# A Strassen feed-forward whose block products are fed in another order on each engine, with a fourth raw weight buffer

## The reference

```python
def swiglu(x, w_in, w_out):
    gate, up = jnp.split(x @ w_in, 2, axis=-1)
    return (jax.nn.silu(gate) * up) @ w_out
```

## Time and profile before

| | |
|---|---|
| time, median of 3 runs | 3603.94 us (3603.62 to 3606.51) |
| profiled execution | 3605.75 us, span 3603.9 us, mean granted clock 0.933 |
| busy share | PE 88%, DVE 55%, ACT 38%, POOL 37% |
| weight transfers, feed-forward inputs | 176 x 512 KB |
| HBM | 251 MB read, 70 GB/s over the span |

### The profile page before, as it was taken

How to read it: one execution, slowest core, us unless ns; L and a number is a source line. 1 busy time by engine, 2 the same in 40 slices (tenths; PEclk the granted TensorE clock), 3 DMA queues, 4 the chain that set the end, 5 groups by cost and what they waited for, 6 DMA issues and landing times.

```text
span 3603.9 us, 50073 instructions
## 1 busy us (share of the span) xinstructions
PE 3179.4 (88%) x20476; PEld 2679.7 (74%) x20476; DVE 1992.3 (55%) x3148; ACT 1383.3 (38%) x2398; POOL 1316.0 (37%) x971
## 2 busy tenths in 40 slices
PE   6999999999997988998998798887888999979787
PEld 4877677777777777866777787877777885678776
DVE  2255483266747464675546645576455617474645
ACT  3331373342643333433444323353233417443323
POOL 2233323335245334263213442424424343353432
PEclk9999999999998999997779899898999999989998
DMA  5212202211021221230001212122121320112222
GB/s 222 88 65 106 93 1 66 94 50 55 19 75 64 81 100 65 77 105 30 8 2 65 80 62 99 64 83 83 70 88 66 98 94 12 53 40 90 77 84 75
DMA packets 74163, 256.73 MB, mean 71 GB/s; under 512 B 8016, under 2 KB 11216, under 8 KB 72784
## 3 DMA queue, kind: packets, MB, share of 16 engines
q1 hardware_dynamic: 73072, 248.82, 20.3%
q0 software_dynamic: 864, 4.72, 0.4%
HBM read 251.41 MB, written 2.10 MB: 70 GB/s over the span
## 4 chain that ended last, share of the span: by engine, by line
PE 61%; DVE 16%; POOL 7%; issue 6%; DMA 5%; ACT 5%; SPq 0%; ACTq 0%; DVEq 0%; POOLq 0%
PE banks L439 59%; DMA w_raw<-in_l_ffn_w_in 4%; DVE area L1502 2%; PE banks L448 2%; POOL w_lo L405 2%; ACT w_hi L390 1%; DVE w_lo L416 1%; DVE w_last L410 1%; DVE w_lo L405 1%; POOL area L1497 1%; POOL w_sum L431 1%; POOL w_sum L425 1%; DVE area L1508 1%; POOL w_sum L429 1%; POOL w_sum L427 1%
## 5 line engine op out<-in xcount | busy, mean ns | idle before, releaser
L439 PE MATMUL banks<-area,w_hi 128*128 128x256 f32 (+3 forms) x6892 | 1709.4, 339 | 215.3 <-ACT area L1449 126.2
L439 PEld LDWEIGHTS banks<-area,w_hi 128*128 128x128 f32 (+2 forms) x6892 | 1195.1, 194 | 396.4 <-ACT area L1449 134.8
L439 PE MATMUL banks<-area,w_lo 128*128 128x256 f32 (+3 forms) x3446 | 1150.7, 336 | 0.0
L405 POOL TENSOR_TENSOR w_lo<-w_raw,w_hi 128x1024 fp32r<-128x1024 f32 (+1 forms) x179 | 416.5, 2329 | 914.5 <-ACT w_hi L390 914.5
L439 PEld LDWEIGHTS banks<-area,w_lo 128*128 128x128 f32 (+2 forms) x3446 | 668.9, 194 | 69.7
L439 PE MATMUL banks<-area,w_late 128*128 128x256 f32 (+2 forms) x2766 | 510.5, 338 | 58.0 <-ACT area L1449 48.7
L439 PEld LDWEIGHTS banks<-area,w_late 128*128 128x128 f32 (+1 forms) x2766 | 428.5, 197 | 119.7 <-ACT area L1449 51.7
L390 ACT ACTIVATE w_hi<-w_raw 128x1024 fp32r<-128x1024 f32 (+2 forms) x271 | 269.5, 1001 | 568.2 <-PE banks L439 282.9
L439 PE MATMUL banks<-area,area 64*64 64x32 f32 (+11 forms) x4424 | 402.4, 316 | 66.3 <-DMA area<-in_w_mod 16.4
L439 PEld LDWEIGHTS banks<-area,area 64*64 64x64 f32 (+4 forms) x4424 | 309.4, 174 | 147.7 <-issue 57.6
L405 POOL TENSOR_TENSOR w_late<-w_raw,w_late 128x1024 fp32r<-128x1024 f32 (+1 forms) x45 | 110.6, 2458 | 324.1 <-ACT w_late L390 324.1
(11 more groups left out here) (286 smaller groups left out, 3708.4 us busy)
## 6 DMA issues: line engine op xcount, KB each, us to landing
w_raw<-in_l_ffn_w_in SPq DMA_DIRECT2D x176, 512.0 KB, 3.4
w_raw<-in_w_in SPq DMA_DIRECT2D x66, 512.0 KB, 3.6
w_raw<-in_l_ffn_w_out SPq DMA_DIRECT2D x64, 512.0 KB, 4.1
w_raw<-in_w_mod SPq DMA_DIRECT2D x32, 512.0 KB, 4.6
w_raw<-in_l_ffn_w_out SPq DMA_DIRECT2D x32, 384.0 KB, 3.1
w_raw<-in_w_qkv SPq DMA_DIRECT2D x24, 512.0 KB, 3.3
w_raw<-in_l_w_in SPq DMA_DIRECT2D x22, 512.0 KB, 3.3
w_raw<-in_w_out SPq DMA_DIRECT2D x32, 320.0 KB, 2.9
```

Source lines behind the costliest of these rows:

```text
L405: e.tensor_tensor(lo, raw_of(m), hi.bitcast(f32), SUB).then_inc(*sig(name, "weights", m, kind))
L439: return e.matmul(out, lhsT, rhs, start=first, stop=stop, skip_group_check=True)
```

## The change

- **Raw buffers.** The angle tables (cos, sin) move to the start of the constants' tile. Once layer 1 has used them for the last time, their 128x1024 serve as a fourth raw buffer; a piece goes to the buffer that was filled longest ago. It is named `const` in the changed kernel.
- **Order of split tiles.** "last" of a unit comes ahead of the next unit's s12 and s34. At a phase's end it comes behind the first output piece; that piece, "last" and the second output piece get their remainders from GpSimd instead of VectorE.
- **ScalarE in a unit.** The p1 copy comes first, then the next unit's gate piece, this unit's s34, silu, u2, "last", the next unit's s12, and the rounding of a.
- **VectorE in a unit.** The s34 remainder moves from the end of the unit before to behind c11; the others follow c22, "last" first.
- **GpSimd.** The fourth sum comes before the third, and the s12 remainder waits for the fourth only. It goes on with the second unit's weights before the last t remainder.
- **Entry of a layer.** VectorE makes two of the t remainders (0 and 1) and both weight remainders before it scales the plain tiles; the third plain tile is worked inside the first unit.
- **Output projection.** All k tiles but the last two, of output tiles 0 and 1, are taken first.

No instruction's size changes. The code (indentation cut by eight, the body of `round_one` is that of the old loop):

```diff
-for _name, _n in (("ident", 128), ("ones", 128), ("head_ones", 128), ("rot", 128), ("eps", 2),
-          ("cos", 512), ("sin", 512), ("upper", 256), ("pick", 128),
+for _name, _n in (("cos", 512), ("sin", 512), ("ident", 128), ("ones", 128), ("head_ones", 128), ("rot", 128), ("eps", 2),
+          ("upper", 256), ("pick", 128),
...
-            ents += [(n, "plain"), (n, "s12")]
-            if ents[-3][1] == "s34":
-                ents.append((ents[-3][0], "last"))
-            ents.append((n, "s34"))
-        elif order[n + 1][0] != name:
-            ents.append((n - 1, "last"))
+            ents.append((n, "plain"))
+            if ents[-2][1] == "s34":
+                ents.append((ents[-2][0], "last"))
+            ents += [(n, "s12"), (n, "s34")]
     elif split:
+        after_units = len(ents) > 0 and ents[-1][1] == "s34"
         ents.append((n, "whole"))
+        if after_units:
+            ents.append((ents[-2][0], "last"))
 ent_at = {ent: k for k, ent in enumerate(ents)}
+end_ents = {k + i for k, (n, kind) in enumerate(ents) if kind == "s34" and ents[k + 1][1] == "whole" for i in (1, 2, 3)}
...
+over_angles = piece_no["l0_ffn1_w_in", 0]
+raw_sb.append(const)
+raw_slots, last_raw = [], [None] * N_RAW
+for n in range(len(order)):
+    if n == over_angles:
+        last_raw.append(None)
+    oldest = min(range(len(last_raw)), key=lambda i: (last_raw[i] is not None, last_raw[i] or 0, i))
+    raw_slots.append((oldest, last_raw[oldest]))
+    last_raw[oldest] = n
+
 def raw_of(n):
-    return raw_sb[n % N_RAW][:, 0:ins[order[n][0]].shape[-1]]
+    return raw_sb[raw_slots[n][0]][:, 0:ins[order[n][0]].shape[-1]]
...
-    if n >= N_RAW:
-        q.wait_ge(*at("raw free", n - N_RAW))
-    e.dma_start(raw_of(n), ins[order[n][0]][order[n][1]]).then_inc(*sig(f"raw{n % N_RAW}", "raw", n, by=16))
+    slot, before = raw_slots[n]
+    if before is not None:
+        q.wait_ge(*at("raw free", before))
+    elif slot == N_RAW:
+        q.wait_ge(*at(layer1.late.tag, "q", "cos", 3))
+        q.wait_ge(*at(layer1.late.tag, "q", "sin", 3))
...
+        round_one(q, e, q.w - 1)
+
+def round_one(q, e, k):
...
-        if kind == "whole" and dve == ("ffn" in order[m][0] or m in last_leads) or (kind == "plain" and not dve):
+        if (kind == "whole" and dve == (("ffn" in order[m][0] or m in last_leads) and k not in end_ents)
+                or (kind == "plain" and not dve)):
...
-        if kind == "last" and dve:
+        if kind == "last" and dve == (k not in end_ents):
...
-            q.wait_ge(*at("weight sums", m, "s34"))
+            q.wait_ge(*at("fourth sum", m))
...
-                e.tensor_tensor(s3, g0, u0, SUB).then_inc(*sig("w_sums"))
                 q.wait_ge(*at("weight sums", m, "s12"))
-                e.tensor_tensor(s4, g1, s2, SUB).then_inc(*sig("w_sums", "weight sums", m, kind))
+                e.tensor_tensor(s4, g1, s2, SUB).then_inc(*sig("w_sums", "fourth sum", m))
+                e.tensor_tensor(s3, g0, u0, SUB).then_inc(*sig("w_sums", "weight sums", m, kind))
...
+            after.t_hi_act(q, e, 0)
         norm.squares.root(q, e, 0)
...
+                lead=[(m, k) for m in range(2) for k in range(j1 - j0 - 2)],
...
-        for i in (0, 1):
-            self.t_hi_act(q, e, i)
-        self.silu_act(q, e, 0)
+        self.t_hi_act(q, e, 1)
+        round_to(q, e, self.ent(DIRECT, "s12"))
         self.t_hi_act(q, e, 2)
-        self.silu_act(q, e, 1)
-        round_to(q, e, self.ent(DIRECT, "s12"))
-        self.a_hi_act(q, e, 0)
-        self.a_hi_act(q, e, 1)
-        self.silu_act(q, e, 2)
-        self.t_hi_act(q, e, 3)
-        round_to(q, e, self.ent(DIRECT, "s34"))
-        self.a_hi_act(q, e, 2)
+        round_to(q, e, self.ent(DIRECT, "s34") + 1)
         for p, out in enumerate(self.outs):
             units = self.units(p)
             for u in units:
                 unit_end = self.ent(u, "s34")
-                more = u < units[-1]
-                if more:
-                    round_to(q, e, unit_end + 1)
                 q.wait_ge(*at(self.tag, "product", u, "p1"))
                 if u - 2 in units:
                     q.wait_ge(*at(self.tag, "c11", u - 2))
                 e.activation(self.p1[u % 2], self.quarter(u, 0), ACT.Copy).then_inc(
                     *sig("ffn_p1", self.tag, "p1", u))
+                if u == DIRECT:
+                    for v in (0, 1):
+                        self.silu_act(q, e, v)
+                else:
+                    round_one(q, e, unit_end + 1)
+                    if q.w <= unit_end:
+                        round_one(q, e, unit_end)
+                    q.w = unit_end + 2
                 if u > units[0]:
                     self.silu_act(q, e, u - 1)
                 q.wait_ge(*at(self.tag, "product", u, "p6"))
@@ -1455,10 +1475,17 @@
                     q.wait_ge(*at(self.tag, "c21", u - 2))
                 e.activation(self.u2[u % 2], self.quarter(u, 0), ACT.Copy).then_inc(
                     *sig("ffn_u2", self.tag, "u2", u))
-                round_to(q, e, unit_end + (3 if more else 1))
+                if u == DIRECT:
+                    for v in (0, 1):
+                        self.a_hi_act(q, e, v)
+                    self.t_hi_act(q, e, 3)
+                round_to(q, e, unit_end + 3)
+                if u == DIRECT:
+                    self.silu_act(q, e, 2)
                 if u > units[0]:
                     self.a_hi_act(q, e, u - 1)
-                round_to(q, e, unit_end + (4 if more else 3))
+                elif u == DIRECT:
+                    self.a_hi_act(q, e, 2)
             self.silu_act(q, e, units[-1])
             self.a_hi_act(q, e, units[-1])
...
+        self.t_lo_dve(q, e, 0)
+        self.last_combined_dve(q, e)
+        self.t_lo_dve(q, e, 1)
+        rest_to(q, e, self.ent(DIRECT, "s34"), dve=True)
         self.norm.scaled(q)
         for u in (0, 1):
             q.wait_ge(*at("evicted", self.project.group(2 * u, 0)))
             e.tensor_tensor(self.sg[u], self.sg[u], self.norm.rs, MUL).then_inc(
                 *sig("lead_scaled", self.tag, "gate", u))
-        self.t_lo_dve(q, e, 0)
         for u in (0, 1):
             q.wait_ge(*at("evicted", self.project.group(2 * u + 1, 0)))
             e.tensor_tensor(self.a[u], self.a[u], self.norm.rs, MUL).then_inc(
                 *sig("lead_scaled", self.tag, "scaled", u))
         for u in (0, 1):
             self.product_dve(q, e, u)
-        self.last_combined_dve(q, e)
-        for u in (0, 1):
-            self.a_lo_dve(q, e, u)
+
+    def third_dve(self, q, e):
+
         q.wait_ge(*at("projected", self.project.group(4, 0)))
         q.wait_ge(*at(self.tag, "product", 0))
         e.tensor_tensor(self.sg[0], self.project.bank(4, 0), self.norm.rs, MUL).then_inc(
             *sig("evicted_dve", "evicted", self.project.group(4, 0)))
         also(self.tag, "gate", 2)
-        rest_to(q, e, self.ent(DIRECT, "s12"), dve=True)
+        self.a_lo_dve(q, e, 0)
         q.wait_ge(*at("projected", self.project.group(5, 0)))
         q.wait_ge(*at(self.tag, "a", 0))
         e.tensor_tensor(self.a[0], self.project.bank(5, 0), self.norm.rs, MUL).then_inc(
             *sig("evicted_dve", "evicted", self.project.group(5, 0)))
         also(self.tag, "scaled", 2)
-        self.product_dve(q, e, 2)
-        rest_to(q, e, self.ent(DIRECT, "s34"), dve=True)
-        self.a_lo_dve(q, e, 2)
+        self.a_lo_dve(q, e, 1)
 
...
-                more = u < units[-1]
...
+                rest_to(q, e, unit_end, dve=True)
...
-                if not more:
-                    rest_to(q, e, unit_end + 1, dve=True)
+                if u == DIRECT:
+                    self.third_dve(q, e)
                 if u > units[0]:
                     self.up_dve(q, e, u - 1)
...
-                rest_to(q, e, unit_end + (3 if more else 2), dve=True)
+                rest_to(q, e, unit_end + 3, dve=True)
                 if u > units[0]:
                     self.a_lo_dve(q, e, u - 1)
-                rest_to(q, e, unit_end + (4 if more else 3), dve=True)
+                elif u == DIRECT:
+                    self.product_dve(q, e, 2)
+                    self.a_lo_dve(q, e, 2)
...
         rest_to(q, e, self.ent(DIRECT, "s34"))
-        for i in (1, 2, 3):
-            self.t_lo_dve(q, e, i, "t_lo_pool")
+        self.t_lo_dve(q, e, 2, "t_lo_pool")
+        rest_to(q, e, self.ent(DIRECT + 1, "s34"))
+        self.t_lo_dve(q, e, 3, "t_lo_pool")
         for p, out in enumerate(self.outs):
-            rest_to(q, e, self.ent(self.units(p)[-1], "last"))
+            rest_to(q, e, self.ent(self.units(p)[-1], "last") + 1)
```

23 lines of the change are left out of this document (12 added, 11 removed).

## The result

The changed kernel takes 3466.6 us (median of 4 runs, 3463.3 to 3471.6) against 3605.2 us for the kernel before beside it: ratio 0.9613, 95% interval [0.9595, 0.9631]. The forecast was 3470. The profiled execution took 3471.55 us (span 3469.8), 134 less than the one before.

The account below looks back on a forecast made before the run. TensorE waits for product 1's copy behind a transfer-bound rounding; afterwards VectorE and GpSimd's shared port bounds units. Savings 28.6 + 0.8 + 3.9 = 33.3 us a layer, 133 in four, give 3470 us; eight-in-ten range 3415 to 3545.

Parts of the forecast that it names:

- entry and phase one: Layer start: entry gains 0.8 us; phase one's copies span 49.8 us (first interval 11.65, then three unit intervals) instead of 56.15.
- phase two: Second group of units in a layer: 9.5 us plus six unit intervals, 85.7 us instead of 99.08.
- phase three: Third group of units in a layer: 9.5 us plus four unit intervals, 60.3 us instead of 69.17.
- output projections (A, B, rest): Last copy of phase one (A) or two (B) to next phase's first, and remaining span: net 1.3 us a phase, 3.9 a layer.
- P: Time of one feed-forward unit in the new order, 12.7 us, between a floor of 11.7 and a ceiling of 15.2.
- 3345 us: Time claimed if VectorE and GpSimd did not exclude each other at the shared port: units of some 10.3 us, time near 3345.
- 12 to 13 us apart: Sign that the forecast is right: the spacing of the product-1 copies in the units.
- other five signs: Copy wait nearly gone; VectorE's 128x1024 remainders often 2 us; TensorE awaits s12, s34; no ScalarE feed-forward transfer waits; entries wait 10 us.
- Both break the loop: Units: fourth raw buffer and product-1 copy ahead of the rounding each break the 15 us transfer loop; the 3.5 us wait goes.
- 4.0 us: First interval of a layer: the new entry order shortens it from 15.65 to 11.65 us.
- with GpSimd splitting the first output tiles the second goes: Output projection start: the second of three TensorE waits, 0.78 us for the first output weights, disappears.
- will often wait a little: Product 7 of a phase's last unit, before the output projection: small waits, allowed for in the net 1.3 us a phase.

Follow-up runs that it names:

- e4: Changed kernel with GpSimd's sum S3 = g0 - u0 replaced by a copy of g0, subtraction left out: ratio 0.9432 to the kernel before; two slow executions not used.
- e8: Changed kernel with the gate piece's 128x1024 remainder on VectorE instead of GpSimd, except in each phase's first unit: 3432.75 us, ratio 0.9521 to the kernel before.
- e3: Kernel before with the fourth raw buffer only, all its orders kept: 3456.61 us, ratio 0.9572 to the kernel before.
- e5: Kernel before with only ScalarE's product-1 copy put ahead of the rounding, three raw buffers: 3611.79 us, ratio 1.0007 to the kernel before.
- e1: Changed kernel with three raw buffers instead of four, all its orders kept: 3503.17 us, ratio 0.9703 to the kernel before.
- e12: Changed kernel with the remainders of a phase's last three pieces back on VectorE: 3445.79 us, ratio 0.9546 to the kernel before.
- e2: Changed kernel without the twelve k steps taken ahead in each output projection: 3465.72 us, ratio 0.9606 to the kernel before.
- e9: Kernel before with the fourth raw buffer and the output projections' twelve k steps ahead, other orders kept: 3442.71 us, ratio 0.9542 to the kernel before.
- e11: Kernel before with the fourth raw buffer, the twelve k steps ahead and the gate piece's remainder on VectorE: 3461.04 us, ratio 0.9592 to the kernel before.

## Why the prediction was right, and where it was not

**The total** came out as forecast, 3466.6 against 3470, but two errors of 7.5 us a layer cancelled in it, so that it is as close as it is by luck. Per layer, forecast and measured:

| | forecast | measured |
|---|---|---|
| entry and phase one | -7.2 (0.8 + 56.15 - 49.8) | -10.4 |
| phase two | -13.4 (99.08 - 85.7) | -16.4 |
| phase three | -8.9 (69.17 - 60.3) | -10.2 |
| output projections (A, B, rest) | -3.9 | +3.5 |
| sum | -33.3 | -33.5 |

**The pace of a unit: right, and shown.** P was forecast as 12.7. Phase two is 83.14 us in the mean of four layers; less its first interval of 8.46 that is 12.45 an interval, and phase three, (58.74 - 8.42)/4, 12.58. The cause was named as the exclusion of VectorE and GpSimd. The fence on two units shows the exclusion, and e4 and e8 that it sets the pace: less time of GpSimd at the port makes the units shorter, by a shorter operation or by moving one to VectorE. No run shortened an operation of VectorE's, and e4's gain is about twice what the port time accounts for. The rule of the Trainium skill that the forecast weighed (SBUF — State Buffer, section SBUF: two separate sides: whichever starts first has the port pair for its whole instruction) is what that fence shows, each record ending about its own length behind the other's, and the 3345 us that stood for the case without it is refuted. Of the 0.3 added to the layout's 12.4 for hand-overs, 0.05 to 0.2 was needed. The first interval of a phase was over-priced by 1.0 us: product 7's wait, for which I had added 1.1, did not lengthen it. The alternation came too, and stronger than in my layout: mostly 9.83 and 13.9 to 15.4 in turn, where I had 10.6 to 14.1. So "12 to 13 us apart" holds for the mean of the copies and for few of them. The other five signs named came out as written, down to the entry's 10 us (53 of the 152 remainders at L436 took 2 us or more).

**Where the words were wrong: what breaks the loop.** The prediction says "Both break the loop". Of the two only the buffer does: e3 has the whole gain and 10 us more, e5 has none. What the prediction did not have is that the other orders shorten the loop by themselves, from 15.0 to 12.9 us with three buffers (e1), so that the time would have been 3503 without the buffer. The step from the longest wait to "the copy no longer stands behind the rounding" took the place where the wait showed for its cause. The transfer was late because its buffer was freed once in 15 us, and with the copy out of the way TensorE waited as long for the remainders.

**Entry.** Most of its gain is not the new order's: e3 has -9.2 with the old order, the changed kernel -10.4. The 4.0 us that I took off the first interval (15.65 to 11.65) for the new order of the entry are there in e3 and e5, which leave the entry as it was: 11.5 in both. The entry's reordering is worth some 1.2 us a layer (not run alone), and I had missed that the buffer helps phase one by more.

**Output projections: the step that failed.** The prediction had "with GpSimd splitting the first output tiles the second goes", net 1.3 a phase. The two waits went, as said, though the second is gone in e12 as well, where VectorE makes these remainders, so GpSimd was not needed for it. But GpSimd's 128x1024 remainders hold the port for 2.25 us each where VectorE's take 1.1, and I did not apply to them the rule that the units were computed with. c22's wait grew from 11.1 (as in e3) to 19.1, which is 0.7 us a phase, and e12 shows that handing them back is worth 2.3 us a phase. The rest of the miss (A is 3.6 us over its forecast) is the last unit of the phase, for which the prediction had "will often wait a little": in A of the second layer TensorE's waits are 1.30, 0.82 and 2.06, 4.2 us together, against 2.5 for the three of rows 7. In the changed kernel the lead's own part is nothing (e2), in the old order 1.1 and 1.3 (e9): somewhat more than the 0.81 of the earlier trace rows that it was to remove.

**What the new orders are worth.** With three buffers they bring 3.0% (e1); on top of the fourth buffer they cost 0.4% (e3 against the changed kernel); and they are needed for the best version, since the gate remainder on VectorE gains in them (e8) and loses without them (e11).

## What to carry to other kernels

The longest wait names an instruction, not a cause: follow it to the resource that is freed once per round, and try that alone before reordering around it. Where VectorE and GpSimd both work between SBUF tiles, count one common timeline: an operation that VectorE does in half the time can be cheaper there even if VectorE is the busier engine (e8), and "give it to the idle GpSimd" at a phase's end cost 2.3 us a phase (e12). But look what the freed engine waits for next: in e8 and e11 it was the transfer. An order that is worth nothing with one assignment of work may be what makes another assignment pay, so test it with both.
